# First attention of a three-block kernel: single heads replaced by pairs of heads in the two halves of the TensorE array, with six score places and a shared scaling

## The reference, cut to what matters

```python
A_HEADS = 16
A_HEAD_DIM = 64
...
        s_own = jnp.einsum('bhqd,bhkd->bhqk', qc, k_own).astype(jnp.float32) * scale
        s_own = jnp.where(k_pos[None, :] <= q_pos[:, None], s_own, NEG)
...
        p = jax.nn.softmax(jnp.concatenate([s_sel, s_own], axis=-1), axis=-1).astype(v.dtype)
```

## Time and profile before

| | us |
|---|---|
| median of 3 runs (lowest, highest) | 1765.5 (1762.85, 1776.5) |
| the profiled execution's own time | 1759.98 |
| its span in the profile | 1758.0 |
| TensorE matmul busy | 1729.1 (98%) |
| VectorE busy | 1108.2 (63%) |
| ScalarE busy | 908.5 (52%) |
| attention's steps, from the scores of head 0 to the first matmul of `w_br_attn` | 207.9 to 346.1 |

### The profile page before, as it was taken

The page is one execution under the profiler, slowest core; times in us unless marked ns, Lnnn a source line. Parts: engine busy times, 40 slices in busy tenths (PEclk is TensorE's granted clock), DMA queues, the critical chain, the costliest instruction groups (busy, mean ns, idle before and its releaser), DMA issues.

```text
span 1758.0 us, 32148 instructions
## 1 busy us (share of the span) xinstructions
PE 1729.1 (98%) x14004; PEld 1661.4 (95%) x14004; DVE 1108.2 (63%) x1487; ACT 908.5 (52%) x1220; POOL 158.5 (9%) x62
## 2 busy tenths in 40 slices
PE   7999999999999999999999999999999999999999
PEld 7999978899999999999988789999999998799999
DVE  6888757565565557765467846555655557756653
ACT  6865577444454445444465545444544446554442
POOL 0000000000022101220000001220122000002210
PEclk9999999999999999999999999999999999999999
DMA  7554332444355455545533205545554564335544
GB/s 271 177 176 146 126 120 97 168 169 167 124 196 187 151 187 206 199 164 180 198 102 133 84 22 195 192 155 185 213 192 170 170 224 136 101 116 195 189 155 134
DMA packets 44635, 284.37 MB, mean 162 GB/s; under 512 B 4944, under 2 KB 6608, under 8 KB 17744
## 3 DMA queue, kind: packets, MB, share of 16 engines
q1 hardware_dynamic: 44352, 282.25, 46.9%
q10 hardware_dynamic: 144, 0.08, 0.0%
HBM read 281.26 MB, written 1.05 MB: 161 GB/s over the span
## 4 chain that ended last, share of the span: by engine, by line
PE 86%; DVE 6%; ACT 5%; issue 2%; DMA 0%; DVEq 0%; ACTq 0%
PE bank L490 85%; ACT WH L1058 2%; DVE WL L1599 2%; ACT SB L1172 0%; DVE HT L1655 0%; ACT SB L1281 0%; DVE STAT L1722 0%; ACT XM L1065 0%; DVE XM L1607 0%; ACT XR L1065 0%; ACT FB L1082 0%; DVE FB L1625 0%; DVE SB L1717 0%; DMA PAR<-in_par 0%; DVE XR L1607 0%
## 5 line engine op out<-in xcount | busy, mean ns | idle before, releaser
L1599 DVE TENSOR_TENSOR WL<-RAW,WH 128x2048 fp32r<-128x2048 f32 (+1 forms) x282 | 590.6, 2096 | 312.0 <-ACT WH L1058 312.0
L490 PE MATMUL bank<-XR,WH 128*128 128x256 f32 x3648 | 651.8, 283 | 11.3 <-DVE WL L1749 10.8
L1058 ACT ACTIVATE WH<-RAW 128x2048 fp32r<-128x2048 f32 (+1 forms) x282 | 493.3, 1752 | 227.7 <-PE bank L490 224.0
L490 PEld LDWEIGHTS bank<-XR,WH 128*128 128x128 f32 x3648 | 561.0, 190 | 17.4 <-DVE WL L1749 10.8
L490 PE MATMUL bank<-XR,WL 128*128 128x256 f32 x1824 | 512.2, 281 | 0.0
L490 PEld LDWEIGHTS bank<-XR,WL 128*128 128x128 f32 x1824 | 346.1, 190 | 0.0
L490 PE MATMUL bank<-XF,WH 128*128 128x256 f32 x1760 | 311.4, 281 | 0.0
L490 PE MATMUL bank<-XM,WH 128*128 128x256 f32 x1664 | 294.7, 281 | 2.7 <-DVE XM L1640 1.6
L490 PEld LDWEIGHTS bank<-XF,WH 128*128 128x128 f32 x1760 | 269.4, 188 | 0.0
L490 PEld LDWEIGHTS bank<-XM,WH 128*128 128x128 f32 x1664 | 254.1, 188 | 4.1 <-DVE XM L1640 2.0
L490 PE MATMUL bank<-XF,WL 128*128 128x256 f32 x880 | 246.9, 281 | 0.0
(11 more groups left out here) (267 smaller groups left out, 1757.4 us busy)
## 6 DMA issues: line engine op xcount, KB each, us to landing
RAW<-in_f1i SPq DMA_DIRECT2D x44, 1024.0 KB, 4.9
RAW<-in_f2i SPq DMA_DIRECT2D x44, 1024.0 KB, 4.9
RAW<-in_w_in SPq DMA_DIRECT2D x35, 1024.0 KB, 4.9
RAW<-in_w_ffn_in SPq DMA_DIRECT2D x22, 1024.0 KB, 4.9
RAW<-in_f1o SPq DMA_DIRECT2D x32, 704.0 KB, 4.1
RAW<-in_f2o SPq DMA_DIRECT2D x32, 704.0 KB, 4.1
RAW<-in_diff_w_in SPq DMA_DIRECT2D x12, 1024.0 KB, 4.9
RAW<-in_w_ffn_out SPq DMA_DIRECT2D x16, 704.0 KB, 4.1
```

The source lines that it names most:

```text
L490: return e.matmul(o, l, r, start=start, stop=stop)
L1058: e.activation(split_at(u, cols)[0], RAW[:, u % NRAW, 0:cols], ACT.Copy).then_inc(hi_done.tick(u), 1)
L1599: e.tensor_tensor(lo, RAW[:, u % NRAW, 0:cols], hi.bitcast(f32), sub).then_inc(lo_done.tick(u), 1)
```

## The change

The attention works on pairs p = 0 to 7 (heads 2p and 2p + 1), in eleven calls instead of twenty. On TensorE a call holds the scores of pair p with the matmuls of its two heads alternating, in two banks; then the product with v of pair p - 3, alternating too; then the turning of both heads of pair p - 2. There are six places for probabilities instead of four; the two new ones lie in `EA`, where the recurrence's products stood before. VectorE takes both heads' scores first, then one maximum instruction over both heads for each of the two column ranges, and it now scales the first 128 columns of each head itself (`settle_pair`); ScalarE scales only the other 256 (`scale_pair`). Calls stand at steps 27, 29, 31, 32, 34, 36, 38, 39, 41, 42 and 43; always ahead of the step's unit on TensorE.

```diff
 BLOCKS = {0: ((0, 64),), 1: ((0, 32), (64, 32))}
-MOBA_STEPS = {29: (0, 1), 30: (2,), 31: (3, 4), 32: (5,), 33: (6, 7), 34: (8,), 35: (9, 10), 36: (11,), 37: (12, 13),
-              **{s: (s - 24,) for s in range(38, 44)}}
+MOBA_STEPS = {27: (0,), 29: (1,), 31: (2,), 32: (3,), 34: (4,), 36: (5,), 38: (6,), 39: (7,), 41: (8,), 42: (9,), 43: (10,)}
...
-        SLOTS = {"moba": [SB[:, n, :] for n in range(4)],
+        SLOTS = {"moba": [SB[:, n, :] for n in range(4)] + [EA[:, n * 384:n * 384 + 384] for n in range(2)],
                  "nsa": [SB[:, n, :] for n in range(4)] + [F(5)[:, 960 + n * 384:1344 + n * 384] for n in range(2)],
                  "diff": [SB[:, n, :] for n in range(4)] + [F(6)[:, n * 384:n * 384 + 384] for n in range(4)]}
+        LATER = {"moba": EA[:, 0:768], "nsa": F(5)[:, 960:1728], "diff": F(6)}
         DIAGS = {"nsa": [F(4)[:, n * 256:n * 256 + 256] for n in range(8)],
                  "diff": [F(7)[:, n * 256:n * 256 + 256] for n in range(8)]}
         def slot(name, i):
             return SLOTS[name][i % len(SLOTS[name])]
+        def pair_slots(name, p):
+            at = 2 * p % len(SLOTS[name])
+            if at < 4:
+                return SB[:, at:at + 2, :]
+            return tiles(LATER[name][:, (at - 4) * 384:(at - 2) * 384], 384)
+        def pair_stat(name, p):
+            return tiles(stat((name, "pair", p), 8), 4)
...
+            def score_pair(name, p, qh, kh, ready):
+                bs = [take("aux", (name, "s", 2 * p + n)) for n in range(2)]
+                for s, k in ready:
+                    q.wait_ge(s, k)
+                for n, b in enumerate(bs):
+                    mm(b[:, 0:128], qh(2 * p + n, 0), kh(2 * p + n)[:, 0:128])
+                for n, b in enumerate(bs):
+                    mm(b[:, 128:384], qh(2 * p + n, 1), kh(2 * p + n)).then_inc(scored.tick((name, 2 * p + n)), 1)
+                for n in range(2):
+                    empties((name, "s", 2 * p + n), (scaled, (name, 2 * p + n)))
+            def weigh_pair(name, p, o, v, start=True, stop=True):
+                ps = [PT[:, pt_slot(name, 2 * p + n), :] for n in range(2)]
+                q.wait_ge(pt_done, (name, 2 * p))
+                q.wait_ge(pt_done, (name, 2 * p + 1))
+                for n in range(2):
+                    mm(o(2 * p + n), v(2 * p + n, 0), ps[n][:, 0:256], start, False)
+                for n in range(2):
+                    mm(o(2 * p + n)[:, 128:256], v(2 * p + n, 1), ps[n][:, 256:384], False, stop).then_inc(weighed.tick((name, 2 * p + n)), 1)
+            def turn_pair(name, p):
+                for i in (2 * p, 2 * p + 1):
+                    b = take("aux", (name, "t", i))
+                    q.wait_ge(first_norm, (name, i))
+                    q.wait_ge(p_norm, (name, i, 1))
+                    for c in range(3):
+                        t = e.transpose(b[:, c * 128:c * 128 + 128], slot(name, i)[:, c * 128:c * 128 + 128], ident)
+                    t.then_inc(posed.tick((name, i)), 1)
+                    empties((name, "t", i), (pt_done, (name, i)))
...
-            def moba(i):
-                if 0 <= i < 16:
-                    scores("moba", i, lambda j: head(QA, i)[:, j * 128:j * 128 + 128], head(KA, i), [(roped, ("ka", 3))])
-                if 0 <= i - 3 < 16:
-                    turn_over("moba", i - 3)
-                h = i - 4
-                if 0 <= h < 16:
-                    if h % 2 == 0:
-                        take("open", ("moba", "o", h // 2))
-                        empties(("moba", "o", h // 2), (pair, ("moba", h // 2)))
-                    rows = h % 2 * 64
+            def moba(p):
+                if p < 8:
+                    score_pair("moba", p, lambda i, j: head(QA, i)[:, j * 128:j * 128 + 128], lambda i: head(KA, i), [(roped, ("ka", 3))])
+                if 0 <= p - 3:
+                    b = take("open", ("moba", "o", p - 3))
+                    empties(("moba", "o", p - 3), (pair, ("moba", p - 3)))
                     for c in range(2):
                         q.wait_ge(copied, ("va", c, 1))
-                    weigh("moba", h, in_bank(("moba", "o", h // 2))[rows:rows + 64, 0:256],
-                          lambda s: tiles(VA, D)[:, s, h * 64:h * 64 + 64])
+                    weigh_pair("moba", p - 3, lambda h: b[h % 2 * 64:h % 2 * 64 + 64, 0:256],
+                               lambda h, s: tiles(VA, D)[:, s, h * 64:h * 64 + 64])
+                if 0 <= p - 2 < 8:
+                    turn_pair("moba", p - 2)
...
+            def score_pair(name, p):
+                st = pair_stat(name, p)
+                q.wait_ge(maxed, (name, "pair", p))
+                for n in range(2):
+                    s = slot(name, 2 * p + n)
+                    for j, (a, z) in enumerate(((0, 128), (128, 384))):
+                        e.activation(s[:, a:z], s[:, a:z], ACT.Exp, scale=slope(name, 2 * p + n), bias=st[:, n, j:j + 1],
+                                     accum_out=st[:, n, 2 + j:3 + j]).then_inc(expd.tick((name, 2 * p + n, j)), 1)
+            def scale_pair(name, p):
+                st = pair_stat(name, p)
+                q.wait_ge(recip, (name, p))
+                for n in range(2):
+                    s = slot(name, 2 * p + n)[:, 128:384]
+                    e.activation(s, s, ACT.Copy, scale=st[:, n, 3:4]).then_inc(p_norm.tick((name, 2 * p + n, 1)), 1)
...
-            def moba(i):
-                if 0 <= i - 3 < 16:
-                    turn_over("moba", i - 3)
-                if 0 <= i < 16:
-                    scores("moba", i)
-                if 0 <= i - 1 < 16:
-                    m = i - 1
-                    s, r = slot("moba", m), stat(("moba", m), 4)[:, 2:4]
-                    q.wait_ge(recip, ("moba", m))
-                    for n, (a, z) in enumerate(((0, 128), (128, 384))):
-                        e.activation(s[:, a:z], s[:, a:z], ACT.Copy, scale=r[:, n:n + 1]).then_inc(p_norm.tick(("moba", m, n)), 1)
+            def moba(p):
+                if 0 <= p - 2 < 8:
+                    turn_over("moba", 2 * p - 4)
+                    turn_over("moba", 2 * p - 3)
+                if p < 8:
+                    score_pair("moba", p)
+                if 0 <= p - 1 < 8:
+                    scale_pair("moba", p - 1)
...
+            def score_pair(name, p):
+                s2, st = pair_slots(name, p), pair_stat(name, p)
+                if 2 * p >= len(SLOTS[name]):
+                    q.wait_ge(posed, (name, 2 * p - len(SLOTS[name]) + 1))
+                for n in range(2):
+                    i = 2 * p + n
+                    q.wait_ge(scored, (name, i))
+                    b = in_bank((name, "s", i))[:, 0:384]
+                    if name == "moba":
+                        e.scalar_tensor_tensor(s2[:, n, :], b, 0.125, con("causal"), mult, add).then_inc(scaled.tick((name, i)), 1)
+                    else:
+                        e.scalar_tensor_tensor(s2[:, n, :], b, 0.125 / slope(name, i), con("dist"), mult, sub).then_inc(scaled.tick((name, i)), 1)
+                q.wait_ge(scaled, (name, 2 * p + 1))
+                for j, (a, z) in enumerate(((0, 128), (128, 384))):
+                    e.tensor_reduce(st[:, :, j], s2[:, :, a:z], X, amax, negate=True).then_inc(maxed.tick((name, "pair", p)), 1)
+                if name == "moba":
+                    return
+                q.wait_ge(maxed, (name, "pair", p))
+                for n in range(2):
+                    e.tensor_scalar(st[:, n, 0:2], st[:, n, 0:2], slope(name, 2 * p + n), None, mult).then_inc(maxed.tick((name, "pair", p)), 1)
+            def settle_pair(name, p, factor=None):
+                s2, r = pair_slots(name, p), pair_stat(name, p)[:, :, 2:4]
+                q.wait_ge(expd, (name, 2 * p + 1, 1))
+                e.reciprocal(r, r).then_inc(recip.tick((name, p)), 1)
+                q.wait_ge(recip, (name, p))
+                if factor is not None:
+                    e.tensor_tensor(r, r, factor, mult).then_inc(recip.tick((name, p)), 1)
+                    q.wait_ge(recip, (name, p))
+                for n in range(2):
+                    s = s2[:, n, 0:128]
+                    e.tensor_scalar(s, s, r[:, n, 0:1], None, mult).then_inc(first_norm.tick((name, 2 * p + n)), 1)
...
-            def moba(i):
-                if 0 <= i < 16:
+            def moba(p):
+                if p < 8:
                     q.wait_ge(small["con"], 0)
-                    scores("moba", i)
-                if 0 <= i - 1 < 16:
-                    settle("moba", i - 1)
-                h = i - 4
-                if 0 <= h < 16 and h % 2 == 1:
-                    q.wait_ge(weighed, ("moba", h))
-                    e.tensor_copy(tiles(OA, 256)[:, h // 2, :], in_bank(("moba", "o", h // 2))[:, 0:256]).then_inc(pair.tick(("moba", h // 2)), 1)
+                    score_pair("moba", p)
+                if 0 <= p - 3:
+                    q.wait_ge(weighed, ("moba", 2 * p - 5))
```

(6 more changed lines are left out.)

## The result

The changed kernel takes 1747.65 us (median of 4 runs, 1745.29 to 1752.07), the kernel before, run beside it, 1764.17 (1759.96 to 1776.5): ratio 0.990, interval 0.986 to 0.994. The forecast was 1749. The profiled execution took 1745.29 us with a span of 1743.5; 1745.0 had been forecast for it.

What follows compares the result with a forecast made beforehand. TensorE, its matmuls filling 98% of the span, was taken as the bound. Less work (14.6 us), ended waits (6.9) and a clock dip (1.7), minus new waits (6.5) and dip (1.7), gave 15.0 us: 1749, range 1745 to 1753.

Steps and rivals of the forecast that it cites:

- Scores in pairs: TensorE's score matmuls: two heads in opposite row halves take 0.86 us, one alone 0.85; saves 5.9 us.
- The rival by which the halves don't overlap: TensorE's alternating matmuls of two halves do not run side by side; 12.1 us of work stay, 1755 us; chance 0.07.
- The product in pairs: TensorE's products with v: two heads in opposite column halves take 0.81 us, one alone 0.79; saves 6.2 us.
- turning: TensorE's transposes, grouped last in a call ahead of the unit, take 5.0 us instead of 7.5; saves 2.5 us.
- The waits of before: TensorE's attention waits, 3.0 us in step 31 and 3.9 elsewhere, go, and the 1.7 us low-clock loss with them.
- 0 to 1 us open: Step 31: allowance for TensorE still waiting on VectorE's copies, which were forecast to end 0.1 us before TensorE arrives.
- Where the new wait comes: Step 39: pair 7's scores need pair 6's banks; TensorE waits 4.8 us, then 1.7; low clock costs 1.7 more.
- the wait for L1233: Step 39: turning pair 5 waits for ScalarE's scaling, which stands behind pair 6's exponentials; 1.7 us.
- The sum: Whole kernel: 23.2 us gross gain less 6.5 of new waits and 1.7 of low clock gives 15.0 us.
- the first: Step 39's wait does not come, since ScalarE gets ahead; 1741 us; chance 0.20.
- the third: ScalarE is 3 us or more later than counted, so unit 36 waits too; 1756 us; chance 0.13.
- the fourth: The pair's chain ends behind TensorE wherever calls stand in adjacent steps; four waits of 6.5 us, 1769 us; chance 0.04.

Runs made afterwards that it cites:

- Both runs on the kernel before: Kernel before, single heads, with no call in step 30, heads 1 and 2 at 29, head 0 at step 28 (1769.15 us) or 27 (1761.13 us).
- the scores ahead: Changed kernel with VectorE's calls of steps 38 and 39 placed ahead of that step's split, memory blocks and merge: 1745.01 us.
- both together: Changed kernel with VectorE's calls of steps 38 and 39 ahead of the split, and pair p - 1 scaled ahead of pair p's scores everywhere: 1743.76 us, ratio 0.986.
- pair 7 later: Changed kernel with the call for pair 7 moved from step 39 to step 40, nothing else: 1748.43 us, ratio 0.993.

## Why the prediction was right

- **Scores in pairs** (5.9 us): right. 0.86 a pair, and the run with one half of the rows takes 1.50. The rival by which the halves don't overlap falls, and with it the question of alternating order.
- **The product in pairs** (6.2) and **turning** (2.5): right. 0.80 and 0.63 for a call, 1.45 with one half of the columns.
- **The waits of before** (6.9 and a dip of 1.7): right in kind. L2051 keeps 0.4 of the "0 to 1 us open", the clock of 230 to 235 is 1.00. Both runs on the kernel before show that the missing call in step 30 does it.
- **Where the new wait comes**: the mechanism was right, and the marks of ScalarE and VectorE were met within 0.6 us. ScalarE's split of unit 34 was forecast at 233.7 and came at 234.2, that of unit 38 at 269.2 and came at 269.65, the split of unit 39 was to end at 280.8 and ended at 281.2, VectorE was to take pair 6's scores at 290.3 and did at 290.84. ScalarE's rows:

```profile
269.65 1.90 ACT L1101 ACTIVATE WH<-RAW 128x2048 fp32r<-128x2048 f32 x1
...
279.40 1.89 ACT L1101 ACTIVATE WH<-RAW 128x2048 fp32r<-128x2048 f32 x1
```

  TensorE's own mark was missed by more: it was to ask for the banks at 286.6 and did at 287.75, of which 0.88 are its two waits of 0.44 us on the way (L2051, L1364). Both marks came late, so that the wait for L1794 is 4.25 for 4.8; the dip is 1.7 for 1.7 of full clock.
- **The term that was mis-sized** is the wait for L1233: 1.7 forecast (the times beside it give 1.6), 0.38 measured. ScalarE was ready at 295.3 where 295.0 had been said; but the sum put TensorE's scores and product at full clock (1.7 us) and then charged a dip behind the wait as well. At the lower level they took 2.96 us, and TensorE came late enough. A dip and the wait inside it must not both be added in full.
- **Left out**: a wait of 0.44 us for L1364, unpriced.
- **The sum**: 23.2 gross, less 5.5 of waits and the 1.5 that the dip cost, is 16.2; w_br_attn starts 16.9 us earlier. The 0.7 us left over lie in TensorE's work, by its busy time in the attention's steps, before (from head 0) and after (from pair 1, to which 0.86 for pair 0 has to be added):

```profile
207.90:346.12 138.22, 131.25 (x944) 113.94 (x944) 84.02 (x140) 92.28 (x188) 0.00 (x0) 0.99 0.35 124
208.77:329.25 120.48, 114.96 (x935) 105.34 (x935) 82.92 (x129) 85.51 (x164) 0.00 (x0) 0.99 0.41 145
```

  131.25 - 115.82 = 15.4 where 14.6 was forecast; which of the three terms is short stays open. The agreement of the profiled execution (1745.29 for 1745.0) is partly luck: w_br_attn came 1.9 us earlier than the forecast's 15.0, and what stands behind it took 2.4 us longer than before (1414.3 against 1411.9), with 6.8 us of full clock missing from 960 to 1000 where the kernel before missed none.
- **Rivals**: the wait came (so not the first), the halves overlap (not the second), unit 36 does not wait (not the third), and there is one such wait and not four (not the fourth). The Trainium skill (TensorEngine Tiling (Array Packing), PSUM Bottleneck) warns that tiling speeds up TensorE and not the emptying of PSUM; in this trace that held at one place, the 4.25 us for L1794, and the cure was VectorE's order, not TensorE's.

## What to carry to other kernels

When matmuls are paired into idle halves of the array, count what the pair asks of the engine that empties the banks: here two heads' scores stood behind two weight splits, and the 4.5 us still to be had came from VectorE's and ScalarE's order alone. Before moving a step in a table, follow the wait around the loop: if ScalarE waits for VectorE's maxima and VectorE for ScalarE's split, moving TensorE's call moves the wait and nothing more. Price a change of 1% in the stretch where it acts, not by the span: in nine further executions of the changed kernel the mean granted clock ran from 0.984 (1764.55 us) to 0.997 (1745.83 us).

## What the runs showed of the hardware

- Eight fp32 matmuls with 64 rows in two opposite row halves take 0.86 us, the same eight in one half 1.50; eight with 64 columns in two column halves of one bank 0.80, in one half 1.45. One head alone (four matmuls) takes 0.85 and 0.79, so the second head is free in the opposite half and costs 0.65 in the same one. Whether the two heads alternate or stand head by head makes no difference (0.86 and 0.81).
- In the attention's stretch a granted clock at its lower level came with every wait of 3.0 to 5.0 us of TensorE, 1.7 or 3.4 us of full clock each time; two executions of the changed kernel show one of each (0.72 and 0.94 from 290 to 300 us, 0.57 and 0.75). Part of it can fall into the wait itself, where it costs nothing. It came nowhere in this stretch with waits of 1.2 us or less alone (the scores ahead, both together), nor with 1.8, 0.8 and 1.2 us within ten microseconds (pair 7 later). Two waits of 0.9 to 1.1 us two microseconds apart were followed by it in both altered kernels before and not in the kernel before itself: what decides that is open.
- From 960 to 1000 us, where TensorE is busy for 39 to 40 of the 40 us, the clock was between 0.70 and 1.00 on different executions, 0 to 12 us. No edit tried here accounts for it, and its cause stays open. The changed kernel's own runs scatter from 1743 to 1765 us, the longer ones at a lower mean clock; whether they lose it at this place no trace shows.
